# A transformer block and four mixer layers on one core: x loaded a second time with the model dimension on partitions, and the first two jobs made panel by panel

## The reference

```python
def _rmsnorm(x, g):
    xf = x.astype(jnp.float32)
    y = xf * lax.rsqrt(jnp.mean(xf * xf, axis=-1, keepdims=True) + EPS)
    return (y * g.astype(jnp.float32)).astype(x.dtype)

def _swiglu(x, w_in, w_out):
    gate, up = jnp.split(x @ w_in, 2, axis=-1)
    return (jax.nn.silu(gate) * up) @ w_out
...
    x = x + 0.5 * _swiglu(_rmsnorm(x, n1_g[l]), ffn1_w_in[l], ffn1_w_out[l])
```

## Time and profile before

| what | value |
|---|---|
| median of three runs | 1737.17 us |
| the three runs | 1736.73, 1737.17, 1737.23 us |
| the profiled execution | span 1734.4 us; the page gives no other time for it, so what lies around the span is taken from the runs: 2.3 to 2.8 us |
| TensorE busy | 1721.4 us |
| VectorE busy | 1183.7 us |
| ScalarE busy | 1040.8 us |
| read from HBM | 308.05 MB |

### The profile page before, as it was taken

One profiled execution on the slowest core, in us unless ns is written; L12 is line 12 of the kernel. 1 busy time (PEld: TensorE's weight loads), 2 busy tenths in 40 slices (PEclk: granted clock), 3 DMA queues, 4 the chain that ended last, 5 costly groups with the idle time before them and its releaser, 6 DMA issues. The chain is left out here.

```text
span 1734.4 us, 22528 instructions
## 1 busy us (share of the span) xinstructions
PE 1721.4 (99%) x8559; PEld 1424.5 (82%) x8559; DVE 1183.7 (68%) x1677; ACT 1040.8 (60%) x1657; POOL 144.5 (8%) x121
## 2 busy tenths in 40 slices
PE   8999999999999999999999999999999999999998
PEld 7888887788888877888888888888888888788887
DVE  6756567677666778766667766588776666786664
ACT  7755567757565766654475744477664446665442
POOL 0000011200000010211000101002011100102110
PEclk9999999999999999999999999999999999999999
DMA  8545454255554533555554555454455545335552
GB/s 323 203 181 197 151 213 146 98 195 200 189 194 161 215 122 122 206 194 184 181 187 169 218 182 191 170 206 147 158 205 185 184 181 193 127 116 222 183 190 73
DMA packets 44987, 310.55 MB, mean 179 GB/s; under 512 B 5232, under 2 KB 5616, under 8 KB 8400
## 3 DMA queue, kind: packets, MB, share of 16 engines
q1 hardware_dynamic: 44464, 307.96, 48.5%
q0 software_dynamic: 272, 1.05, 0.2%
q10 hardware_dynamic: 144, 0.11, 0.0%
HBM read 308.05 MB, written 1.05 MB: 178 GB/s over the span
## 5 line engine op out<-in xcount | busy, mean ns | idle before, releaser
L1286 DVE SCALAR_TENSOR_TENSOR wlo<-raw,first,whi 128x512 fp32r<-128x512 f32 x704 | 501.8, 775 | 120.2 <-ACT whi L695 119.6
L695 ACT ACTIVATE whi<-raw,first 128x512 fp32r<-128x512 f32 x704 | 450.1, 714 | 104.8 <-PE ps L2117 84.2
L2115 PE MATMUL ps<-whi,xs 128*128 128x512 f32 (+1 forms) x1184 | 472.7, 399 | 1.1 <-DVE wlo L1286 0.9
L2117 PE MATMUL ps<-whi,xs 128*128 128x512 f32 (+1 forms) x1184 | 461.0, 389 | 0.0
L2116 PE MATMUL ps<-wlo,xs 128*128 128x512 f32 (+1 forms) x1184 | 460.0, 388 | 0.0
L1283 DVE TENSOR_TENSOR wlo<-raw,whi 128x2048 fp32r<-128x2048 f32 x110 | 251.7, 2307 | 68.5 <-ACT whi L690 68.3
L2115 PE MATMUL ps<-whi,hhi 128*128 128x512 f32 x720 | 282.4, 392 | 0.0
L2117 PE MATMUL ps<-whi,hlo 128*128 128x512 f32 x720 | 280.6, 390 | 0.0
L2116 PE MATMUL ps<-wlo,hhi 128*128 128x512 f32 x720 | 280.4, 389 | 0.0
L2204 PE MATMUL ps<-xs,whi 128*128 128x512 f32 x768 | 273.0, 399 | 0.0
L2115 PEld LDWEIGHTS ps<-whi,xs 128*128 128x128 f32 x1184 | 222.4, 188 | 48.9 <-issue 3.9
(11 more groups left out here) (235 smaller groups left out, 1306.4 us busy)
## 6 DMA issues: line engine op xcount, KB each, us to landing
raw<-in_w_parts SPq DMA_DIRECT2D x285, 1024.0 KB, 4.8
gain<-in_gains SPq DMA_DIRECT2D x10, 512.0 KB, 6.3
x<-in_x SPq DMA_DIRECT2D x2, 512.0 KB, 6.4
raw<-in_w_parts SPq DMA_DIRECT2D x2, 512.0 KB, 5.8
arena<-in_bias_line POOLq DMA_DIRECT2D x1, 1024.0 KB, 11.9
out<-x SPq DMA_DIRECT2D x4, 256.0 KB, 2.1
const<-in_const_in SPq DMA_DIRECT2D x1, 288.0 KB, 13.1
wup<-in_gla_up SPq DMA_DIRECT2D x1, 192.0 KB, 12.4
```

Source lines behind the costliest of these rows:

```text
L695: nc.scalar.activation(whi[n % HIS][:, cols], raw[n % LOS][:, cols], ACT.Copy, scale=gcol[:, COLUMNS[n] + kk:COLUMNS[n] + kk + 1]).then_in ...
L1286: nc.vector.scalar_tensor_tensor(out=lo[:, cols], in0=whole[:, cols], scalar=gcol[:, COLUMNS[n] + kk:COLUMNS[n] + kk + 1], in1=hi[:, cols] ...
L2115: nc.tensor.matmul(out_ap, a_hi, wh, start=first, stop=False)
L2117: return nc.tensor.matmul(out_ap, a_lo, wh, start=False, stop=last)
```

## The change

x comes a second time from the host as `x_turned`, [128, 8, 256], that is with the model dimension on partitions. It is loaded in two pieces (panels 0 and 1, then 2 to 7) around the first half of part 0, into space of `proj` that is free. xhi and xlo of the first stage are made from it, two panels and both token tiles at a time, between the splits of parts 0 and 1. The eight transposes of each tile fall away, and with them the nine of `keep_clock`; in their place VectorE clears 128 columns and TensorE makes ten products of zeros (`warm_clock`). `jobs_by_panel` makes job (0,0) and (0,1) together, panel by panel, then (1,0) and (1,1) in the same way. x by rows, for the squares and the sums, is loaded after part 2. Both squares come after the splits of part 3. gcol and the identity are loaded as two DMAs with a semaphore each, and VectorE and TensorE don't wait for them at the start.

```diff
@@ -156,6 +157,7 @@
+        s["by_panel"] = i == 1
@@ -183,6 +185,11 @@
+def job_at(s, j, t):
+
+    return NT * j + t + 1 if s["by_panel"] else nth_job(j, t)
...
@@ -616,7 +627,9 @@
                 if n == 0:
+                    sp.dma_start(X_TURNED[:, 0:2, :], x_turned[:, 0:2, :]).then_inc(x_turned_in[0], 16)
                     sp.dma_start(raw[0][:, 0:PART // 2], w_parts[0, :, 0:PART // 2]).then_inc(half_in, 16)
+                    sp.dma_start(X_TURNED[:, 2:KT, :], x_turned[:, 2:KT, :]).then_inc(x_turned_in[1], 16)
                     sp.dma_start(raw[0][:, PART // 2:PART], w_parts[0, :, PART // 2:PART]).then_inc(raw_in[0], 16)
@@ -653,8 +666,9 @@
-                        if n in (0, 2):
-                            load_x(n // 2)
+                        if n == 3:
+                            for t in range(NT):
+                                load_x(t)
@@ -679,7 +693,8 @@
-            act.dma_start(first[:], first_in).then_inc(first_in_sem, 16)
+            act.dma_start(gcol, first_in[:, P:P + TOTAL["column"] * KT]).then_inc(gcol_in, 16)
+            act.dma_start(ident, first_in[:, 0:P]).then_inc(first_in_sem, 16)
@@ -723,7 +736,7 @@
                     act.wait_ge(norm_ready, s["norms"])
-                    act.wait_ge(job_done, s["n_job"] + nth_job(i, t))
+                    act.wait_ge(job_done, s["n_job"] + job_at(s, i, t))
@@ -842,7 +855,29 @@
+            def first_bound(s, part):
+
+                for b in range(KT // 2):
+                    if b < 2:
+                        act.wait_ge(x_turned_in[b], 16)
+                    nc.scalar.activation(xhi[:, 2 * b:2 * b + 2, :], X_TURNED[:, 2 * b:2 * b + 2, :], ACT.Copy).then_inc(xhi_ready, 1)
+                    if b == 0:
+                        act.wait_ge(gcol_in, 16)
+                    hi_to(b // 2, 2 * (b % 2) + 2)
+                hi_to(part + 4)
+                for t in range(NT):
+                    act.wait_ge(x_tile_in[t], 16)
+                    ins = squares(t, ROW_NORM + t)
+                ins.then_inc(sum_ready, 1)
+                hi_to(part + 5)
+                root(stat, ROW_NORM, ROW_NORM + NT, s["n_var"])
+                act.wait_ge(suffix_in_sem, 16)
+                nc.scalar.activation(suffix[:], SUFFIX_STAGE, ACT.Copy).then_inc(suffix_ready, 1)
@@ -1288,7 +1317,7 @@
-            dve.wait_ge(first_in_sem, 16)
+            nc.vector.memset(arena[:, 0:P], 0.0).then_inc(warm_ready, 1)
@@ -1324,8 +1353,30 @@
+            def first_bound(s, part):
+
+                for b in range(KT // 2):
+                    dve.wait_ge(xhi_ready, b + 1)
+                    nc.vector.tensor_tensor(xlo[:, 2 * b:2 * b + 2, :], X_TURNED[:, 2 * b:2 * b + 2, :],
+                                            xhi[:, 2 * b:2 * b + 2, :].bitcast(F32), ALU.subtract).then_inc(xlo_ready, 1)
+                    lo_to(b // 2, 2 * (b % 2) + 2)
+                lo_to(part + 4)
+                c = slice(ROW_NORM, ROW_NORM + NT)
+                mean_square(stat, ROW_NORM, ROW_NORM + NT, s["n_chain"])
+                lo_to(part + 5)
+                newton(stat, ROW_NORM, ROW_NORM + NT, s["n_chain"])
...
@@ -2099,14 +2143,11 @@
-            pe.wait_ge(first_in_sem, 16)
-
-            def keep_clock(bank, n):
+            def warm_clock(n):
+
+                pe.wait_ge(warm_ready, 1)
                 for _ in range(n):
-                    nc.tensor.transpose(ps[:, bank, SPAN:SPAN + P], ident, ident)
+                    nc.tensor.matmul(ps[:, 7, 0:P], arena[:, 0:P], arena[:, 0:P], start=True, stop=True)
@@ -2140,9 +2181,31 @@
+            def jobs_by_panel(bank_of, parts_of):
+
+                for i in range(2):
+                    for j, n in enumerate(parts_of(i)):
+                        for kk in range(PANELS):
+                            k = j * PANELS + kk
+                            if i == 0 and k % 2 == 0:
+                                pe.wait_ge(xlo_ready, k // 2 + 1)
+                            weights(n, kk)
+                            for t in range(NT):
+                                ins = split_mm(ps[:, bank_of(i, t), :], xhi[:, k, t * P:(t + 1) * P], xlo[:, k, t * P:(t + 1) * P],
+                                               n, kk, k == 0, k == KT - 1)
+                                if k == KT - 1:
+                                    ins.then_inc(job_done, 1)
+                        if j == 0:
+                            ins.then_inc(w_used, 1)
+
             def first_jobs(s, bank_of, parts_of):
 
                 turn = s["turns_here"]
+                if s["by_panel"]:
+                    warm_clock(WARM)
+                    jobs_by_panel(bank_of, parts_of)
+                    pe.wait_ge(first_in_sem, 16)
+                    return
@@ -2157,10 +2220,6 @@
-                if turn["add"] is None:
-                    for half in range(2):
-                        turn_half(turn, 0, half)
-                    keep_clock(6, 9)
```

More of the change, by code:

```diff
@@ L25 @@
 FAR = -1.0e30
+WARM = 10
 TAKEN = -3.0e38
@@ L114, in stage_list @@
         if kind == "turn" or kind == "bound" and s["turn"]:
-            run["tr"] += 1
+            run["tr"] += kind == "turn" or s["add"] is not None
             run["xt"] += 1
@@ L199, in parts_freed @@
                     by_use(parts[0])
-                    freed[parts[1]] = ("job_done", s["n_job"] + nth_job(i, NT - 1))
+                    freed[parts[1]] = ("job_done", s["n_job"] + job_at(s, i, NT - 1))
                 else:
@@ L267, in sb_columns, with build @@
     return np.concatenate([v[:, 0:512], q[:, 0:512], k[:, 0:512], q[:, 512:], k[:, 512:], v[:, 512:]], 1)
-def build(nc, x_in, w_parts, gains, first_in, const_in, suffix_in, bias_line, conv_w, gla_low, gla_up, gla_b, out):
+def build(nc, x_in, x_turned, w_parts, gains, first_in, const_in, suffix_in, bias_line, conv_w, gla_low, gla_up, gla_b, out):
     STAGES, TOTAL = stage_list()
@@ L335, in build @@
         SUFFIX_STAGE = proj[:, 0, 0:2 * P]
+        X_TURNED = proj[:, 1, 0:KT * SEQ].rearrange("p (k n) -> p k n", k=KT)
         GE, ONES = suffix[:, 0:P], suffix[:, P:2 * P]
@@ L395, in build @@
         first_in_sem = sem("first_in")
+        gcol_in = sem("gcol_in")
+        x_turned_in = [sem("x_turned_in0"), sem("x_turned_in1")]
+        warm_ready = sem("warm_ready")
         half_in = sem("half_in")
@@ L696, in split_hi @@
                                          scale=gcol[:, COLUMNS[n] + kk:COLUMNS[n] + kk + 1]).then_inc(hi_ready, 1)
-            act.wait_ge(first_in_sem, 16)
             def hi_to(end, panels=0):
@@ L843, in squares @@
                 return nc.scalar.activation(JUNK[t], x[:, t, :], ACT.Square, scale=D ** -0.5, accum_out=stat[:, 0, col:col + 1])
+            def first_bound(s, part):
[15 more added lines that the diff above has]
+                nc.scalar.activation(suffix[:], SUFFIX_STAGE, ACT.Copy).then_inc(suffix_ready, 1)
             def bound(s, part):
+                if s["add"] is None:
+                    first_bound(s, part)
+                    return
                 for t in range(NT):
@@ L863, in bound @@
                     if s["turn"]:
-                        if t == 1 or s["add"] is not None:
-                            hi_to(part + (4 if t == 1 else 3 if s["final"] else 2))
+                        hi_to(part + (4 if t == 1 else 3 if s["final"] else 2))
                         for half in range(2):
                             turned_hi(s, t, half)
-                        if s["add"] is None:
-                            hi_to(part + 2 + 2 * t)
                         ins = squares(t, ROW_NORM + t)
@@ L875, in bound @@
                     root(stat, ROW_NORM, ROW_NORM + NT, s["n_var"] + (NT if s["final"] else 0))
-                if s["add"] is None:
-                    act.wait_ge(suffix_in_sem, 16)
-                    nc.scalar.activation(suffix[:], SUFFIX_STAGE, ACT.Copy).then_inc(suffix_ready, 1)
             def copy_t(base, b, scale=1.0, dst=None):
@@ L1325, in turned_lo @@
                     turned_lo_half(s, t, half)
+            def first_bound(s, part):
[9 more added lines that the diff above has]
+                newton(stat, ROW_NORM, ROW_NORM + NT, s["n_chain"])
+                nc.vector.tensor_scalar(stat[:, NEG_RS, c], stat[:, RS, c], -1.0, None, ALU.mult).then_inc(norm_ready, 1)
+                dve.wait_ge(const_sem, 16)
+                dve.wait_ge(small_sem, 64)
+                c = (GLA_NORM - 1) * KT
+                nc.vector.tensor_tensor(wlow[:], wlow[:], gcol[:, c:c + KT].unsqueeze(2).to_broadcast([P, KT, 16]), ALU.mult
+                                        ).then_inc(low_gained, 1)
             def bound(s, part):
                 chain, q = s["n_chain"], s["n_gain"]
+                if s["add"] is None:
+                    first_bound(s, part)
+                    return
                 def halves(update):
@@ L1376, in bound @@
                         halves(plus_normed_sum)
-                    elif s["add"] is not None:
+                    else:
```

(6 more changed lines are left out.)

## The result

The changed kernel takes 1739.31 us (median of 21 runs, 1738.31 to 1741.14) against 1736.97 us for the kernel before in the same comparison (21 runs, 1736.45 to 1737.42): ratio 1.0015, 95% interval 1.0009 to 1.0021, that is 1.6 to 3.6 us. It is 2.3 us slower, inside the stated range; the forecast was 1.1. The span of the profiled execution, one of the lower ones at 1738.92 us, is 1736.8 us against 1734.4.

A forecast was written before the change was run, and what follows sets the result against it. TensorE, 99% busy, was taken to bound the kernel. 3.2 us won early, less stops of 1.1, 3.1 and 0.1 us, left it 1.1 us slower: 1738.3 us, range 1735.2 to 1740.5.

The forecast's parts named there:

- What bounds the kernel: Whole span: TensorE is busy 99%, so only some 13 us of idle time can be won and delays reaching it count.
- Start: First product on TensorE at 7.25 us instead of 8.93: 1.7 us won.
- the running sum: Landing times from summed DMA GB/s plus some 0.85 us lag; it put raw0's first half at 5.6 us.
- The products of zeros: At the start, ten products at 2.12 / 9 us a piece, ending by about 3.6 us, long before 7.25.
- The stop before up(2,0): After the four first jobs end at 29.8 us, TensorE waits 1.1 us for the gate of (0,0), at 30.9.
- the stop before panel 2: Early in the first jobs, TensorE stops 0.8 us after two panels for raw0's second half.
- raw3 and raw4: With 1.05 MB more ahead of raw3, part 4's whi starts at 24.1 us instead of 21.60, 2.5 us late.
- the step at the transposes: TensorE waits 3.1 us for the gate of (1,1); the last hidden transposes start at 39.8 against 38.7 us.
- The rest of the chain is untouched, 15.6 us: ScalarE and VectorE, from part 4's whi to the end of (1,1)'s gate: still 15.6 us, so ready at 39.7.
- the chain isn't late: Rival: raw4's landing hardly depends on x and part 4 is split no later; 1.5 us faster, 1735.7; chance 0.10.
- The bounds: Rates of the first 6 us and the clock unknown: the net change could be +0.1 to +2.1 us.
- The clock rival: A TensorE pause of 3 us or more at 36.6 us halves the clock: +3.4 us, 1740.6; chance 0.14.

The follow-up runs named there:

- e10: The changed kernel with 18 products of zeros at the start instead of 10: 1739.23 us.
- e9: The changed kernel again, unchanged, on the chip of the later runs: 1740.30 us, in two groups of times.
- e2: The changed kernel with x by rows loaded only after part 5 and the squares made from x_turned's space: 1739.61 us.
- e5: The changed kernel with the squares before the splits of part 3 and root and Newton step right behind them, so an early norm: 1739.56 us.
- e8: The changed kernel with activations and gates in the order (0,0), (0,1), splits of part 5, (1,0), (1,1): 1736.60 us.
- e3: The changed kernel with 26 products of zeros at the start instead of 10: 1740.39 us.
- e1: The kernel before, with x loaded by rows once more (1.05 MB, unused) ahead of raw3: 1738.38 us, 1.4 above before.
- e6: The changed kernel with the activation order of e8 and the early norm of e5 together: 1735.11 us, ratio to before 0.9989.
- e7: e6 with 18 products of zeros at the start instead of 10: 1733.92 us, ratio to before 0.9981.

## Why the prediction was right, and where it was off

**What bounds the kernel, right.** TensorE is 99% busy; all that the change gave or took lies in its idle time and in its clock.

**Start, right in kind.** The first product came 1.15 us sooner, not 1.7: the first half of raw0 lands 0.5 us later than the running sum gave. The low clock from 8.1 to 11.4 us was called harmless, and e10 bears it out: without it TensorE waits 1.8 us more before up(2,0), and the lower times are the same.

**The products of zeros, mis-sized.** Priced like transposes at 0.235 us, they are two matmuls each: 0.42 us.

**The stop before up(2,0), wrong.** The sum had 1.1 us there; it is 0.17. The four jobs end near 31.2 us, not 29.8: 0.5 us for the later start and some 1.6 for the slow products, less the 0.8 us of the stop before panel 2, which did not come about. The sum had the low clock only as a remark. It costs nothing, since up(2,0) could not have started before the gate of (0,0), 31.47 us.

**raw3 and raw4, right.** Forecast 2.5 us late, measured 24.66 - 21.60 = 3.1. This 0.6 us is most of what the step at the transposes missed: up(2,1) is 1.7 us late, not 1.1.

**What the stop comes from, right as far as it went.** I foresaw the place (the transposes of tile 1), the gate that ends it and about its size (3.1 us against 2.4; up(2,0) and its two transposes took 6.4 us, not 5.7). "The rest of the chain is untouched, 15.6 us" held: 40.24 - 24.66 = 15.6. What I did not see is a second condition close below the first. In the kernel before, job (1,0) ended near 22 us, long before its activation's turn came; made panel by panel its last product ends at 30.7, and the activation, which started at 31.59 behind the gate of (0,0), had only some 0.8 us to spare over it. In e9's execution it even started behind the job (31.75 us, after its last product ended at 31.66). That the number came out near is therefore partly luck: the forecast has no term for this, and with the loads in time (e2) or the norm early (e5) up(2,1) is still 0.9 and 0.7 us late. For the same reason the rival "the chain isn't late" was priced wrongly at 1.5 us faster: with raw4 in time TensorE can't start up(2,1) before some 39.5 to 39.7 us. And the chain's length was taken as given, though 2.3 us of it are the two waits for gates, which e8 removes.

**The bounds and what can be measured.** 2.3 us lies just above the +2.1 of the bounds, inside a range that also took in part of the clock case. The prediction put what can be told from no change at 3.5 us; the interval of 21 runs a side, 1.6 to 3.6 us, does not contain zero.

**The clock rival, right as a mechanism.** It came true in e9's profiled execution, and probably in 8 of the 21 runs of the comparison, those above 1740 us, which no profile shows. Its price was lower, 1.7 us for 2.3, since I took the length of the slow stretch from the start of the kernel. I had made it depend on a pause of 3 us; 2.4 us was enough, though not in every execution. The Trainium skill, "TensorE: Matmul & The Clock Gate", section "Why this matters for your kernels", warns against idle gaps between bursts of matmuls; the traces of e9, e2, e3 and e10 agree, while those of the changed kernel and e5 have the same stop and the full clock behind it.

**What nobody foresaw.** 0.6 us at 1169 us, in the gated linear attention: TensorE waits for `hlo` of the low-rank gate, VectorE and ScalarE being late after a part that landed late (ScalarE is idle for 1.34 us for it at 1163.84 in the changed kernel; the kernel before splits the eight panels from 1158.32 us on without a wait between them).

Together, for the profiled execution: 1.7 + 0.6 = 2.3, of a span that is 2.4 longer. The median of the runs lies 0.4 above this execution; that some runs have the slow clock would explain it.

## What to carry to other kernels

When the producer's order is changed (two tiles together instead of one after the other), change the consumers' order with it: what the earlier order let finish early now finishes late, and a fixed order of activations turns that into a stop however well the loads are timed. Where one consumer must wait for another on the same tile's scratch space, let the tiles alternate: that took 2.5 us out of this chain (e8). Price a chain from all the things that start it, not from the one that is late now, and ask what the next one is. And count the bytes that a second copy of an input puts ahead of each later load: they cost here 1.4 us by themselves in the kernel before (e1), and left no wait of TensorE at this place once the work that waits for them had been moved away from the path (e6, e7).

## What the runs showed of the hardware

Six profiles have a stop of 2.4 us of TensorE before the transposes. In four of them (e2, e3, e9, e10) the granted clock fell to 0.50 for some 3.4 us behind it, 1.6 to 1.7 us of time; in two (the changed kernel, e5) it did not. At the start, idle times of 1.9 to 2.7 us before the first product were followed by products 0.43 us apart in all six profiles that have them (the changed kernel, e2, e5, e6, e8, e9). With 18 products of zeros, which leave 0.66 us, the products came at full pace at once (e10).

The granted clock of a window need not show this: in e9 it reads 1.00 from 8 to 12.5 us, while the products come 0.43 us apart. The distance between products is the safer sign.

A product of two plain float32 tiles of 128x128 is two matmuls in the record. Ten took 4.2 us at the start of the changed kernel, slower than later ones: in e10 7 or 8 matmuls fall into each microsecond from 2 to 5 us, and 12 and 10 into the next two.

The wait of 0.5 to 0.9 us near 1170 us is in all six profiles that have slow products at the start (the changed kernel, e2, e5, e6, e8, e9) and in none of the five without them (before, e1, e3, e7, e10). e10's expectation had named both outcomes, and the wait was absent, as the rule has it; by what way the first microseconds should reach a load a thousand microseconds later stays open. So does the later raw4 of e3 and e10.
